# A routed expert layer on one core: expert weights fetched in 2 MB transfers and handed over by halves

## The reference

```python
logits = (h @ w_router + b_router).astype(jnp.float32)
top_val, top_exp = lax.top_k(logits, TOP_K)          # 4 of 32 experts for each token
gate_w = jax.nn.softmax(top_val, axis=-1)
...
def expert_block(args):
    xb, e = args
    gt = jnp.minimum(xb @ w_gate[e] + b_gate[e], SWIGLU_LIMIT)
    up = jnp.clip(xb @ w_up[e] + b_up[e], -SWIGLU_LIMIT, SWIGLU_LIMIT)
    return (gt * jax.nn.sigmoid(SWIGLU_ALPHA * gt) * (up + 1.0)) @ w_down[e] + b_down[e]
...
y = jax.ops.segment_sum(y_pad[dest] * sorted_w[:, None].astype(h.dtype), sorted_tok, num_segments=T)
```

## Time and profile before

| | us |
|---|---|
| median of 3 runs (1550.06 to 1554.86) | 1551.28 |
| profiled execution, its own time | 1550.92 |
| its span, first to last instruction | 1548.6 |
| PE busy | 1339.2 |
| DVE busy | 789.7 |
| PE idle in front of gate and up matmuls | 122.3 |
| packets of SP's queue, share of the 16 DMA engines' span | 76.3% |

### The profile page before, as it was taken

How to read it: one execution, slowest core, us unless ns; L and a number is a source line. 1 busy time by engine, 2 the same in 40 slices (tenths; PEclk the granted TensorE clock), 3 DMA queues, 4 the chain that set the end, 5 groups by cost and what they waited for, 6 DMA issues and landing times. The chain is left out here.

```text
span 1548.6 us, 37446 instructions
## 1 busy us (share of the span) xinstructions
PE 1339.2 (86%) x13050; PEld 566.9 (37%) x13051; DVE 789.7 (51%) x2773; ACT 197.9 (13%) x522; POOL 279.6 (18%) x214
## 2 busy tenths in 40 slices
PE   7999988989969874998899899796996999799852
PEld 3444445455443321332233333232332343233311
DVE  1219694555778663454355544443553455355414
ACT  0112235554010000000000000000000000000002
POOL 0001000103521210221122212121221122122201
PEclk9999979999969986999899999997998899999976
DMA  9831074663193999979997999989899799999995
GB/s 343 235 94 62 1 235 137 243 217 150 68 374 146 406 417 418 386 296 416 406 408 303 411 409 410 389 319 413 302 405 418 291 411 408 415 397 406 412 416 220
DMA packets 124843, 488.27 MB, mean 315 GB/s; under 512 B 35955, under 2 KB 54971, under 8 KB 74620
## 3 DMA queue, kind: packets, MB, share of 16 engines
q1 hardware_dynamic: 108668, 470.84, 76.3%
q0 software_dynamic: 16128, 16.82, 5.1%
HBM read 474.40 MB, written 17.77 MB: 318 GB/s over the span
## 5 line engine op out<-in xcount | busy, mean ns | idle before, releaser
L1087 PE MATMUL banks<-arena,misc 128*32 128x512 f32 x5248 | 630.3, 620 | 122.3 <-DMA arena<-in_w_up 109.6
L1087 PEld LDWEIGHTS banks<-arena,misc 128*32 128x32 f32 x5248 | 168.8, 113 | 485.3 <-issue 309.5
L1097 PE MATMUL banks<-arena,master 128*32 128x256 f32 x5248 | 321.5, 386 | 2.6 <-DVE banks L1771 2.2
L1844 DVE TENSOR_SCALAR cst<-banks 128x256 f32<-128x256 f32 x82 | 34.8, 425 | 378.5 <-PE banks L1087 375.3
L1097 PEld LDWEIGHTS banks<-arena,master 128*32 128x32 f32 x5248 | 165.0, 112 | 145.5 <-issue 61.5
L679 POOL DMA_INDIRECT misc<-moe_input,misc x84 | 88.4, 1052 | 656.8 <-DVE misc L1745 626.7
L695 POOL DMA_INDIRECT moe_output<-misc x82 | 130.2, 1588 | 205.3 <-issue 199.5
L1329 ACT ACTIVATE banks<-cst 128x256 f32<-128x256 f32 x82 | 31.8, 388 | 1009.5 <-DVE cst L1844 1009.5
L847 PE MATMUL banks<-arena 128*128 128x512 f32 x256 | 112.6, 595 | 0.0
L1511 DVE CUSTOM_DVE_ANT_0 arena<-banks,master 128x128 f32<-128x128 f32 (+3 forms) x96 | 46.0, 480 | 59.3 <-PE banks L947 55.8
L1716 DVE SCALAR_TENSOR_TENSOR master<-banks,cbias 128x512 bf16<-128x512 f32 x85 | 63.8, 750 | 13.1 <-issue 4.1
(11 more groups left out here) (376 smaller groups left out, 1119.6 us busy)
## 6 DMA issues: line engine op xcount, KB each, us to landing
arena<-in_w_gate SPq DMA_DIRECT2D x128, 1024.0 KB, 15.4
arena<-in_w_up SPq DMA_DIRECT2D x128, 1024.0 KB, 17.6
arena<-in_w_down SPq DMA_DIRECT2D x128, 1024.0 KB, 17.6
arena<-in_w_ada SPq DMA_DIRECT2D x12, 2048.0 KB, 12.9
arena<-in_w_in SPq DMA_DIRECT2D x2, 2048.0 KB, 10.7
master<-bias_by_distance SPq DMA_DIRECT2D x16, 256.0 KB, 4.4
arena<-in_w_in SPq DMA_DIRECT2D x8, 256.0 KB, 4.4
arena<-in_cmp_k_w SPq DMA_DIRECT2D x2, 1024.0 KB, 6.1
```

The source lines that it names most:

```text
L1087: last = nc.tensor.matmul(two(bank[2 * b][strip(j), :]), hTe[:, k, :], pair[:, :, k % 2, quarter(j)], start=False, stop=(k == KC - 1), ski ...
L1097: last = nc.tensor.matmul(bank[2 * b + 1][strip(j), 0:256], actT[:, q, c, :], DN(b, q, c)[:, quarter(j)], start=False, stop=(q == 3 and c ...
```

## The change

Gate, up and down each come in two halves of four neighbouring rows for each partition, so one transfer is 2 MB and its contiguous run in a partition is 16 KB instead of 8 KB. Half 0 of gate and up is k = 0 to 3, half 1 is k = 4 to 7. The bytes and their order in the queue stay as they are. PE waits for weights at k = 0 and k = 4, and at q = 0 and q = 2. SP begins to refill gate and up after k = 3 (`done7` now adds 3, not 1), takes the second half after k = 7, the first half of down after q = 1 and the second after q = 3. The bias row of the last layer norm (`ln2b`) moves from row 26 to row 28 of `arena`.

```diff
-                rows2 = slice(first + 4 * i + 2 * m, first + 4 * i + 2 * m + 2) if type(first) is int else ds(first + (4 * i + 2 * m), 2)
-                src = a["w_up" if m else "w_gate"][0, e].rearrange("a (p i k) n -> i p (a k) n", i=KC // 2, k=2)[i]
-                sp.dma_start(arena[:, rows2, :], src).then_inc(s_wg[i], 16)
+                rows4 = slice(first + 8 * i + 4 * m, first + 8 * i + 4 * m + 4) if type(first) is int else ds(first + (8 * i + 4 * m), 4)
+                src = a["w_up" if m else "w_gate"][0, e].rearrange("a (p i k) n -> i p (a k) n", i=2, k=4)[i]
+                sp.dma_start(arena[:, rows4, :], src).then_inc(s_wg[i], 16)
...
-                for i in range(KC // 2):
-                    if i == KC // 2 - 1:
+                for i in range(2):
+                    if i:
                         sp.wait_ge(s_a, done)
-                    elif i:
-                        sp.wait_ge(s_gu, done7 + 2 * i)
                     sp.wait_ge(s_wg[i], x * 32)
                     for m in range(2):
                         gate_up_load(i, e, first, m)
...
-                for q in range(4):
-                    if q == 3:
-                        sp.wait_ge(s_c, done + 1)
-                    elif q:
-                        sp.wait_ge(s_dn, done * 3 + q)
-                    sp.wait_ge(s_wd[q], x * 16)
-                    down_load(q, e, first)
+                sp.wait_ge(s_dn, done * 3 + 1)
+                sp.wait_ge(s_wd[0], x * 16)
+                down_load(0, e, first)
+                sp.wait_ge(s_c, done + 1)
+                sp.wait_ge(s_wd[1], x * 16)
+                down_load(1, e, first)
...
-                if k % 2 == 0:
-                    pe.wait_ge(s_wg[k // 2], landed)
+                if k % 4 == 0:
+                    pe.wait_ge(s_wg[k // 4], landed)
...
-                pe.wait_ge(s_wd[q], landed)
+                if q % 2 == 0:
+                    pe.wait_ge(s_wd[q // 2], landed)
...
-                nc.vector.tensor_scalar(done7_i[v][0:1, :], done7_i[v][0:1, :], 1.0, None, ALU.add)
+                nc.vector.tensor_scalar(done7_i[v][0:1, :], done7_i[v][0:1, :], 3.0, None, ALU.add)
```

More of the change, by code:

```diff
@@ L171, in build_layer @@
         g1r, sc2r, sh2r, ln1g, ln1b = rows[0:5]
-        ln2g, ln2b = arena[:, 24, :], arena[:, 26, :]
+        ln2g, ln2b = arena[:, 24, :], arena[:, 28, :]
         x1 = xn
@@ L310, in build_layer @@
         s_free, s_open = sem("ring_part_free"), sem("expert_banks_open")
-        s_wg = [sem(f"gate_up_pair{i}_loaded") for i in range(KC // 2)]
-        s_wd = [sem(f"down{q}_loaded") for q in range(4)]
+        s_wg = [sem(f"gate_up_half{i}_loaded") for i in range(2)]
+        s_wd = [sem(f"down_half{i}_loaded") for i in range(2)]
         s_wdb = sem("second_down_loaded")
@@ L478, in _ @@
             sp.wait_ge(s_quart, 4)
-            for i in range(2):
-                for m in range(2):
-                    gate_up_load(i, eA, 0, m)
+            for m in range(2):
+                gate_up_load(0, eA, 0, m)
             sp.wait_ge(s_quart, 5)
@@ L505, in second @@
             def second(i):
-                if i < 2:
+                if i < 1:
                     sp.wait_ge(s_wg[i], 32)
@@ L510, in second @@
                     gate_up_load(i, eB, 24, m)
-            for i in (2, 3):
-                second(i)
+            second(1)
             def rows_out(q):
@@ L526, in _ @@
             sp.wait_ge(s_free, 1)
[L527 to L530, removed]
+            sp.wait_ge(s_wg[1], 32)
+            for m in range(2):
+                gate_up_load(1, eA, 0, m)
             bias_load(s_bg, 0, 512, eA, 0)
@@ L533, in _ @@
             rows_out(3)
-            for i in range(2):
-                second(i)
+            second(0)
             sp.wait_ge(s_bg, 16)
@@ L542, in _ @@
             sp.wait_ge(s_rT, QT)
[L543 to L546, removed]
+            down_load(0, eA, 0)
+            down_load(0, eB, 24, s_wdb)
             sp.wait_ge(s_zst, 16 * QT)
-            for q in (2, 3):
-                down_load(q, eB, 24, s_wdb)
+            down_load(1, eB, 24, s_wdb)
             sp.wait_ge(s_below, 1)
-            for q in (2, 3):
-                down_load(q, eA, 0)
-            sp.wait_ge(s_wdb, 64)
-            for q in range(4):
-                sp.wait_ge(s_wd[q], 16)
-                sp.sem_inc(s_wd[q], 16)
+            down_load(1, eA, 0)
+            sp.wait_ge(s_wdb, 32)
+            for i in range(2):
+                sp.wait_ge(s_wd[i], 16)
+                sp.sem_inc(s_wd[i], 16)
             sp.wait_ge(s_tables, 1)
@@ L563, in reload @@
                 done = sp.value_load(done_i[v][0:1, ds(x, 1)], min_val=1, max_val=NX)
[L564 removed]
+                done7 = sp.value_load(done7_i[v][0:1, ds(x, 1)], min_val=10, max_val=7 * NX + 3)
                 b = sp.value_load(base_i[v][0:1, ds(x, 1)], min_val=0, max_val=1)
@@ L1081, in gate_up @@
             def gate_up(b, k, landed):
-                if k % 2 == 0:
-                    pe.wait_ge(s_wg[k // 2], landed)
-                pair = arena[:, 24 * b + 4 * (k // 2):24 * b + 4 * (k // 2) + 4, :].rearrange("p (m r) n -> p m r n", m=2)
+                if k % 4 == 0:
+                    pe.wait_ge(s_wg[k // 4], landed)
+                half = arena[:, 24 * b + 8 * (k // 4):24 * b + 8 * (k // 4) + 8, :].rearrange("p (m r) n -> p m r n", m=2)
                 for j in range(4):
                     last = nc.tensor.matmul(two(bank[2 * b][strip(j), :]), hTe[:, k, :],
-                                            pair[:, :, k % 2, quarter(j)],
+                                            half[:, :, k % 4, quarter(j)],
                                             start=False, stop=(k == KC - 1), skip_group_check=True)
```

9 lines of the change are left out of this document (4 added, 5 removed).

## The result

The changed kernel takes 1646.36 us (median of 4 runs, 1645.57 to 1647.51), the kernel before 1551.17 us beside it (1550.06 to 1554.86). The ratio is 1.062, with a 95% interval from 1.060 to 1.063: 95 us slower. The forecast was 1585 us, so the sign and the wide range held and the size did not: 34 us were forecast, 95 came.

What follows compares the result with a forecast made beforehand. PE and the DMA weight stream were taken to bound the kernel by turns. From 1550.9 us, packets -16, restarts +8.9 and arrivals +21 (+14 together), then the ring +20, gave 1585 us; own range 1570 to 1605, overall 1556 to 1685.

Steps and rivals of the forecast that it cites:

- The late release: At a reload's restart, SP's first bytes wait for k = 3 instead of k = 1: 1.78 us later each.
- the early need: When PE waits for the stream, work once done before the last arrival now follows it: k = 6 is 3.5 us later.
- all five restarts on the path end a pause: Five restarts of the weight stream have nothing to cover their later release: 5 x 1.78 = 8.9 us added.
- the six arrivals: Ends of the six stream stretches, where PE waits for the last part: 3.5 us each, 21 us added.
- a stretch of PE: One of five stretches between those of the stream, where PE was taken as the bound and faster packets save nothing.
- the six lengths: Durations of the six stretches where the weight stream sets the pace, the first given as 153.8 us, 803 us in sum.
- the clock after a wait: TensorE's lower 1.2 GHz clock after idling: only in the upper bound for arrivals, 7 us each, 42 in all.
- packets: In the weight stream, 16 KB packets for two of 8 KB save 2% of 803 us: 16 us.
- the ring: Small transfers wait longer behind larger packets; late scatters make items 13.1 instead of 10.65 us at PE's pace: 20 us.
- The one in which all time behind the stream scales: Rival: the scatter's 4.6 us behind the stream become 9.2, the loop 15.3 us, total 1674 us; chance 0.27.
- Handovers only: Rival: small transfers don't mind larger packets and only the handovers count, 1565 us; chance 0.18.
- A far faster stream: Rival: fewer, larger packets speed the weight stream by 5% to 7%, 1541 us; chance 0.10.

Runs made afterwards that it cites:

- the three kernels with 8 KB runs: The kernel before with transfers unchanged and handovers by halves: SP's release only 1569.63 us, PE's waits only 1612.68 us, both sides 1658.89 us.
- the run with both by halves: The kernel before, 1 MB transfers in 8 KB runs kept, with SP's releases and PE's waits both by halves: 1658.89 us, ratio 1.070.
- the first-half kernel: The kernel before with gate and up's first half and all of down in 2 MB transfers, the second half still in pairs: 1567.95 us, ratio 1.011.
- The small scatter: The changed kernel with a scatter moving only the first 16 of each item's 128 rows: 1603.33 us, ratio 1.035 against the kernel before.

## Why the prediction was right or wrong

**Right: the direction, and both prices of a handover.** The late release (1.78 us) and the early need (3.5 us) are the right sizes: they and one spare time fit the three kernels with 8 KB runs. SP's first load came after k = 3; PE waited at k = 0 and 4; a row of 16, a row of 32 and k = 6 followed at once.

**Wrong: how often they are paid.** The step that failed is "all five restarts on the path end a pause" and "the six arrivals", with "the later handovers cost nothing while a backlog covers them". I counted 5 and 6, 8.9 + 21 = 30 us; the run with both by halves cost 108.7 us, as if some 25 reloads each paid the delay less 1 us. (In fact 15 of them lost 5.8 us each and 11 lost 1.6.) The error was in the reading. PE never idle was taken for "PE is the bound", and the rest for slack. But from 672 to 835 us the stream did not pause either. Both were full, and the last pair landed as PE reached k = 6. The backlog was what the tight handover had built up: with the release later and the need earlier, the 8.4 MB of gate and up no longer fit into their window (24.8 us of work in 21.0, where there were 26.1), and the stream runs dry at sixteen reloads where it did at five. The trace of before would have said so: 26.8 us from SP's start at 798.40 to k = 6 at 825.16, in the middle of what I called a stretch of PE (755.22 on), with a wait of 0.61 us at its end. (The first of the six lengths is 154.15 us and not 153.8, which changes nothing.)

**Missed: the clock after a wait.** The 1.8 us of slower work behind each new wait at k = 4 stood in the prediction only as an upper bound. In the turn shown they are a third of what a reload at PE's pace lost on average (5.67 us).

**About right: packets.** 16 us were forecast; the changed kernel is 12.5 us faster than the one with the same handovers and small packets, and the first-half kernel shows 17 in its reloads. From 500 to 1500 us a packet of 16 KB took 611 ns in the median, two of 8 KB 618: 1.1% less, where 2% was taken. But down alone in large packets showed nothing.

**Right in mechanism, wrong in effect: the ring.** The scatters came 12.9 us apart where 13.1 was forecast, and DVE waited 1.94 and then 4.22 us for them:

```profile
797.32 0.15 DVE L1741 CAST misc<-misc 128x1 uint32<-128x1 f32 x1 [1.94 <-DMA moe_output<-misc]
...
800.97 0.43 DVE L1834 TENSOR_SCALAR cst<-banks 128x256 f32<-128x256 f32 x1 [1.85 <-PE banks L1076]
...
810.23 0.15 DVE L1741 CAST misc<-misc 128x1 uint32<-128x1 f32 x1 [4.22 <-DMA moe_output<-misc]
...
817.34 0.42 DVE L1834 TENSOR_SCALAR cst<-banks 128x256 f32<-128x256 f32 x1 [5.32 <-PE banks L1076]
```

```profile
798.91 1.59 POOL L684 DMA_INDIRECT moe_output<-misc  x1 [4.51 <-issue]
...
811.82 1.59 POOL L684 DMA_INDIRECT moe_output<-misc  x1 [6.77 <-issue]
```

From its issue at 798.91 to DVE's pass at 810.23 the scatter took 11.3 us, where it was 9.1 before: 2.2 more, against the 2.4 of the eight turns. Its first packet came 4.8 us after the issue in both kernels, and from there to the end of its last packet it was 3.8 us before and 5.9 after. But DVE still idles before each activation, and the item with a reload, 16.37 us long, gives it all its slack back. The 20 us were worked out for eight items in a row at PE's pace, and such rows no longer exist. The handovers' loss hid the ring's, and the kernel whose handovers are finer pays it, 17 us. The turns by packet that the prediction worked with, weighed against the Trainium skill's "DMA: Bandwidth & Descriptors", section "Queues, rings and completion order", agree with this: only kernels with 16 KB runs show long waits for the scatter (137.3, 182.5 and 206.9 us, and 62.7 with down alone), those with 8 KB don't (7.2 to 15.7). The page counts as a packet a group of some 9 to 17 descriptors, and the traces count single runs, so they don't show that the two are the same thing.

**The rivals.** The one in which all time behind the stream scales came nearest by number, 1674, and is wrong: PE's waits are for weights, not behind the scatter, and the time ahead of a scatter's first packet did not grow. "Handovers only" had the right mechanism, but took its count, five and six, from the forecast. A far faster stream was not seen.

Why SP's bias and 8.4 MB take 24.8 us, when 8.4 MB at 408 GB/s take 20.6, is settled for the most part. The bias takes 0.9. From 786.34 to 810.21 (23.87 us) the queues of the changed kernel had (packets, MB, share of the 16 engines):

```profile
q1 hardware_dynamic: 615, 8.78, 89.7%
q0 software_dynamic: 362, 0.41, 8.4%
```

That is 21.4 us of the engines' time for weights, 20.5 of them for gate and up and 0.9 for 0.4 MB of down that went through beside them, and 2.0 for the small transfers: 24.3 of the 24.8 us with the bias. The small scatter agrees: it shortened the 15 intervals by 2.4 us each, on average. No kernel that does the whole work beats the one before.

## What to carry to other kernels

An engine that never waits is no proof of slack behind it: for each repeated handover measure from release to need, and compare with when the data landed; a margin of 0 to 1 us at every turn means that each further delay is paid at every such turn, nearly in full. A larger transfer is released later and needed earlier by its own grain, at both ends, and the two delays share one spare time, so one edit can look cheap and the pair be dear. Price a change that has several costs together: here the handovers' loss hid that of the ring, which came forth in the kernel whose handovers were better.

## What the runs showed of the hardware

- The scatters weigh more on the stream than I had thought. Their 112 rows less in each of some 80 items took the small transfers' queue from 5.1% of the 16 engines' span (79 us) to 2.1% (32 us), and 31 us of time came back in the kernel before. In the changed kernel it was 43, but there the shorter ring may have a part in it. The queue's row with 16 rows a scatter, in the kernel before:

```profile
q0 software_dynamic: 6944, 9.60, 2.1%
```

- Runs of 16 KB are carried as packets of 16 KB; with the same handovers they made the program 0.8% faster, and the changed kernel's full slices reach 420 to 423 GB/s.
- Behind PE's wait of 3.8 us the work is slower, with the granted clock at 0.78 and 0.59 in the two rows that follow: the next 16 products took 2.48 us instead of 1.90, and the 32 after them 3.11 instead of 1.91.
